# Input and first constants loaded ahead of the vector rows, group-norm fill split, and GpSimd making two of four key rows of the gate matrices

## What is computed

```python
x = first_block(x, ...)      # 2 layers: rms_norm, four branches, gates, MLP
return second_block(x, ...)  # 2 layers: modulated norm, mixer, PEER experts
```

```python
mean = jnp.mean(y, -1, keepdims=True)
var = jnp.mean(jnp.square(y - mean), -1, keepdims=True)
y = (y - mean) * lax.rsqrt(var + RWKV_GN_EPS) * hv(ln_g) + hv(ln_b)
```

```python
expert = jnp.take_along_axis(cand_idx, pos, axis=-1)
gates = jax.nn.softmax(top, axis=-1)
act = gelu(einsum('td,ted->te', hc, u[ec]))
out = einsum('te,ted->td', (gc * act), v[ec])
```

## Time and profile before

| what | us |
|---|---|
| median of 3 runs (lowest, highest) | 4231.68 (4229.45, 4231.91) |
| the profiled execution's own time | 4230.72 |
| its span in the trace | 4228.9 |
| PE busy | 4002.5 (95%) |
| DVE busy | 2099.7 (50%) |
| ACT busy | 1470.3 (35%) |
| POOL busy | 156.3 (4%) |
| mean granted clock of PE | 0.97 |

### The profile page before, as it was taken

One profiled execution on the slowest core, in us unless ns is written; L12 is line 12 of the kernel. 1 busy time (PEld: TensorE's weight loads), 2 busy tenths in 40 slices (PEclk: granted clock), 3 DMA queues, 4 the chain that ended last, 5 costly groups with the idle time before them and its releaser, 6 DMA issues.

```text
span 4228.9 us, 66869 instructions
## 1 busy us (share of the span) xinstructions
PE 4002.5 (95%) x24777; PEld 3561.0 (84%) x24777; DVE 2099.7 (50%) x4725; ACT 1470.3 (35%) x3017; POOL 156.3 (4%) x214
## 2 busy tenths in 40 slices
PE   7999989999999899899999999999989999999999
PEld 5887879979788799788887888888868878898888
DVE  1334324414343254533299555555531995555555
ACT  1222115421221163311234444444432344444444
POOL 3100100040001000000000000000000000000000
PEclk9998999999989999999999999999999999999999
DMA  4562235545512356437341555445523515554443
GB/s 129 125 177 71 58 90 150 172 122 135 167 55 61 105 160 173 102 95 195 106 137 47 182 170 175 169 170 170 151 81 107 147 46 173 174 170 170 170 173 123
DMA packets 652676, 565.62 MB, mean 134 GB/s; under 512 B 56491, under 2 KB 585786, under 8 KB 652090
## 3 DMA queue, kind: packets, MB, share of 16 engines
q1 hardware_dynamic: 652122, 559.67, 43.9%
q0 software_dynamic: 352, 3.15, 0.2%
HBM read 553.30 MB, written 9.44 MB: 133 GB/s over the span
## 4 chain that ended last, share of the span: by engine, by line
PE 89%; DVE 7%; ACT 2%; issue 1%; SPq 0%; DVEq 0%; DMA 0%; ACTq 0%
PE bank L705 22%; PE bank L1138 13%; PE bank L725 9%; PE bank L1152 6%; PE bank L1153 6%; PE bank L1151 6%; PE bank L1091 5%; PE bank L794 4%; PE bank L1127 4%; PE bank L1105 2%; PE bank L701 2%; DVE uT L2582 1%; PE bank L1081 1%; PE bank L888 1%; PE bank L898 1%; PE bank L750 1%
## 5 line engine op out<-in xcount | busy, mean ns | idle before, releaser
L705 PE MATMUL bank<-hT,ring 128*128 128x256 f32 (+1 forms) x3184 | 721.5, 387 | 23.2 <-ACT hT L1370 16.2
L705 PEld LDWEIGHTS bank<-hT,ring 128*128 128x128 f32 (+1 forms) x3184 | 609.1, 192 | 121.1 <-issue 30.9
L1138 PE MATMUL bank<-h_high,u_parts 128*128 128x256 f32 x3072 | 437.9, 285 | 0.0
L2593 DVE TENSOR_TENSOR u_parts<-bank,u_parts 128x512 fp32r<-128x512 f32 x384 | 247.0, 685 | 327.4 <-ACT u_parts L1659 327.4
L1151 PE MATMUL bank<-v_high,w_low 128*128 128x512 f32 x1024 | 406.7, 397 | 0.4 <-DVE v_low L2614 0.4
L1152 PE MATMUL bank<-v_low,w_high 128*128 128x512 f32 x1024 | 405.9, 396 | 0.0
L1153 PE MATMUL bank<-v_high,w_high 128*128 128x512 f32 x1024 | 404.8, 395 | 0.0
L1138 PEld LDWEIGHTS bank<-h_high,u_parts 128*128 128x128 f32 x3072 | 395.5, 189 | 5.9
L1360 ACT ACTIVATE arena<-bank 128x256 f32<-128x256 f32 (+2 forms) x326 | 125.1, 387 | 714.2 <-PE bank L705 545.4
L2614 DVE TENSOR_TENSOR v_low<-ring,v_high 128x512 fp32r<-128x512 f32 x512 | 336.9, 689 | 65.6 <-ACT v_high L1676 41.5
L705 PE MATMUL bank<-arena,ring 128*128 128x256 f32 (+2 forms) x1216 | 295.3, 397 | 45.6 <-DVE arena L2309 28.8
(11 more groups left out here) (391 smaller groups left out, 5847.4 us busy)
## 6 DMA issues: line engine op xcount, KB each, us to landing
ring<-in_peer_u SPq DMA_DIRECT2D x256, 512.0 KB, 4.2
ring<-in_peer_v SPq DMA_DIRECT2D x256, 512.0 KB, 3.5
ring<-in_w_in SPq DMA_DIRECT2D x132, 512.0 KB, 3.8
ring<-in_mod_w SPq DMA_DIRECT2D x96, 512.0 KB, 4.3
ring<-in_mlp_up SPq DMA_DIRECT2D x64, 512.0 KB, 4.0
ring<-in_mlp_down SPq DMA_DIRECT2D x64, 512.0 KB, 4.1
ring<-in_w_branch SPq DMA_DIRECT2D x64, 256.0 KB, 2.8
ring<-in_peer_w_q SPq DMA_DIRECT2D x32, 512.0 KB, 3.9
```

Source lines behind the costliest of these rows:

```text
L705: ins = eng.matmul(ps[0:n, 0:width], wv[:, i, :], moving(u * 8 + i), start=(u == 0 and i == 0), stop=(u == count - 1 and i == k - 1))
L1138: ins = eng.matmul(PB[6 + b][:, 0:S], u_parts[:, part, k * P:k * P + P], moving[:, k, :], start=(n == 0), stop=(n == len(products) - 1))
L2593: tt_(u_parts[:, 1, d], PB[4 + q][:, :], u_parts[:, 0, d].bitcast(F32), ALU.subtract).then_inc(sem("uL_ready"), 1)
```

## The change

Three things are changed. (1) At the start, SP loads the first 384 columns of the constants and the input, in two halves, with a semaphore of their own (`x_in`); 28 of the 49 rows are issued by SP behind them, the other 21 by ACT; the first four weight units come next, and the positions and the other constants last (`tables_in`). PE turns the input as soon as `x_in` is there, DVE copies it out bank by bank, ACT squares it, and the rows are turned last. DVE waits for the rows (`vec_ready`) only before it scales. (2) In `group_norm`, PE runs one label of fill before the second product and the rest behind it; in the RWKV branch ACT takes the root after four labels, not after all. (3) In the gate matrices, DVE compares only two of the four tokens' key rows, and POOL makes the other two, in two operations of 128x128 with a semaphore of their own (`pool_rows`). Several semaphores of another branch are also joined under one name, with the same waits.

```diff
         ANGLES, SINES, COSINES = (8, 14), (10, 16), (12, 18)
+        FILL_SQUARE, FILL_ROOT = 1, 3
...
-        SETUP = 4 + DEPTH * (12 + len(SHIFTED) + 3) + 7
+        SETUP = DEPTH * (12 + len(SHIFTED) + 3) + 7
+        FIRST_CONSTS = 3 * P
...
                 ins.then_inc(sem("gn_sum"), 1)
-                for label in fill:
+                for label in islice(fill, FILL_SQUARE):
                     project(label)
...
                 ins.then_inc(sem("gn_var"), 1)
+                for label in fill:
+                    project(label)
...
             def start_up():
-                eng.wait_ge(sem("setup_in"), pe.next("setup_in", 16 * SETUP))
+                eng.wait_ge(sem("x_in"), 16 * 3)
+                for k in range(KD):
+                    for tt in range(TT):
+                        ins = eng.transpose(PB[k // 2][:, (k % 2) * S + tt * P:(k % 2) * S + tt * P + P],
+                                            x_in[:, tt, k * P:k * P + P], C("ident"))
+                    if k % 2:
+                        ins.then_inc(sem("x_turned"), 1)
+                eng.wait_ge(sem("setup_in"), 16 * SETUP)
                 for i in range(4):
-                    eng.transpose(PB[0][:, i * P:i * P + P], rows_in[:, i, :], C("ident"))
...
+                    ins = eng.transpose(PB[6][:, i * P:i * P + P], rows_in[:, i, :], C("ident"))
...
                     eng.wait_ge(sem("one_rows"), n + (1 + base))
+                    eng.wait_ge(sem("pool_rows"), n + (1 + base))
...
+                for label in islice(fill, FILL_SQUARE + FILL_ROOT):
+                    projected(label)
+                root(gn_rs)
                 for label in fill:
                     projected(label)
-                root(gn_rs)
...
+            eng.wait_ge(sem("rows_zero"), 1)
+            layer_rows(eng, 1)
+            for b in range(4):
+                eng.wait_ge(sem("x_ready"), act.next("x_ready"))
+                eng.activation(square[:, 2 * b:2 * b + 2, :], xT[:, 2 * b:2 * b + 2, :], ACT.Square).then_inc(sem("sq_ready"), 2)
...
+            def gate_rows(l):
+
+                base = 64 * l
+                eng.wait_ge(sem("pickT_ev"), l + 1)
+                for n in range(64):
+                    b = n % 2
+                    if n >= 2:
+                        eng.wait_ge(sem("pool_rows"), n - 1 + base)
+                        eng.wait_ge(sem("gate_mm"), n - 1 + base)
+                    for j in range(2, 4):
+                        at = slice(n * 4 + j, n * 4 + j + 1)
+                        ins = ts_(one_p[:, b, j, :], C("iota"), selT[:, 1, at], None, ALU.is_equal)
+                    ins.then_inc(sem("pool_rows"), 1)
...
+            eng.dma_start(cst[:, 0:FIRST_CONSTS], io["consts"][:, 0:FIRST_CONSTS]).then_inc(sem("x_in"), 16)
+            for tt in range(TT):
+                eng.dma_start(x_in[:, tt, :], io["x"][0, tt * P:tt * P + P, :]).then_inc(sem("x_in"), 16)
             eng.wait_ge(sem("rows_zero"), 1)
+            layer_rows(eng, 0)
+            other_rows(eng)
+            load_units(4)
+            for i, name in enumerate(("positions", "positions_2")):
+                table(ipos[:, i, :], io[name].to_broadcast([P, S]))
+            table(cst[:, FIRST_CONSTS:], io["consts"][:, FIRST_CONSTS:])
...
-                    tt_(one_p[:, b, :, :], C("iota").unsqueeze(1).to_broadcast([P, 4, NKEY]),
-                        selT[:, 1, four].unsqueeze(2).to_broadcast([P, 4, NKEY]), ALU.is_equal)
+                    tt_(one_p[:, b, 0:2, :], C("iota").unsqueeze(1).to_broadcast([P, 2, NKEY]),
+                        selT[:, 1, two].unsqueeze(2).to_broadcast([P, 2, NKEY]), ALU.is_equal)
...
+            for b in range(4):
+                eng.wait_ge(sem("x_turned"), b + 1)
+                eng.tensor_copy(xT[:, 2 * b:2 * b + 2, :].rearrange("p a b -> p (a b)"), PB[b][:, :]).then_inc(sem("x_ready"), 1)
```

More of the change, by code:

```diff
@@ L1257, in gdn @@
                 eng.wait_ge(sem("go_ev"), pe.uses["go_ev"])
-                eng.wait_ge(sem("go_sq"), pe.next("go_sq"))
+                eng.wait_ge(sem("gdn_sq"), pe.next("gdn_sq"))
                 for h in range(4):
@@ L1591, in gdn @@
                     eng.wait_ge(sem("go_ev"), act.next("go_ev"))
-                eng.activation(gsq[:, 0:4, :], mix_t[:, 0:4, :], ACT.Square).then_inc(sem("go_sq"), 1)
+                eng.activation(gsq[:, 0:4, :], mix_t[:, 0:4, :], ACT.Square).then_inc(sem("gdn_sq"), 1)
                 root(gsq[:, 0:4, :])
@@ L1705, in _ @@
                 if l == 0:
+                    eng.wait_ge(sem("vec_ready"), act.next("vec_ready"))
+                    eng.activation(cond, vec[:, 3, VEC3["c"][0]:VEC3["c"][0] + 8], ACT.Silu).then_inc(sem("vec_ready"), 1)
                     sines(0)
@@ L1861, in _ @@
             condition()
+            for l in range(DEPTH):
+                gate_rows(l)
         @block.sync
@@ L2380, in gdn @@
                 eng.wait_ge(sem("gdn_scalar_in"), dve.next("gdn_scalar_in"))
[L2381 removed]
+                eng.wait_ge(sem("gdn_exps"), dve.next("gdn_exps"))
                 tt_(sp_t[:, 2, :, :], sp_t[:, 2, :, :], sp_t[:, 1, :, :], ALU.add).then_inc(sem("dve_step"), 1)
@@ L2411, in gdn @@
                 eng.wait_ge(sem("gdn_tensor_in"), dve.next("gdn_tensor_in"))
-                eng.wait_ge(sem("erow_ready"), dve.next("erow_ready"))
+                eng.wait_ge(sem("gdn_exps"), dve.next("gdn_exps", 2))
                 for b in range(8):
@@ L2573, in gate_rows @@
                 for n in range(64):
-                    b, four = n % 2, slice(n * 4, n * 4 + 4)
+                    b, two = n % 2, slice(n * 4, n * 4 + 2)
                     if n >= 2:
```

98 lines of the change are left out of this document (42 added, 56 removed).

## The result

| | before | changed |
|---|---|---|
| median | 4231.8 us | 4162.6 us |
| lowest to highest | 4229.5 to 4231.9 | 4156.6 to 4166.7 (4 executions) |
| profiled execution, its own time | 4230.7 | 4166.7 |
| its span | 4228.9 | 4164.9 |

The ratio is 0.9837, with a 95% interval of 0.9818 to 0.9856: the kernel became faster by 1.6%. The forecast was 4248 us, slower. In a second series of five executions of the changed kernel the median was 4161.8 us, with a ratio of 0.9835 (0.9821 to 0.9848). Two executions stand far apart and are left out of the ratios: one of the kernel before, of 6519.2 us (left out of the range above too), and one of five of the run with both norms as before, of 4249.5 us at a mean granted clock of 0.923.

A forecast was written before the change was run, and what follows sets the result against it. PE, busy for 95% of the span, was taken as the bound, so edits count only where it waits. 4230.7 - 14.5 - 28.8 - 5.2 - 3.4 + 69 gave 4248 us; range 4172 to 4322.

The forecast's parts named there:

- The start: Before the first projection: rows landing 7.1 us earlier plus 7.4 us of input work done beforehand, -14.5 us; bounds -10 and -15.
- The RWKV norm: Group norm of the RWKV branch, two layers: PE's 14.39 us wait goes, -28.8 us, and half clock behind it, -5.2 us.
- Retention: Retention's group norm: PE's 2.28 us wait for the root shrinks by 1.7 us per layer, -3.4 us; bounds 0 and -4.6.
- The gate stage: Gate matrices, 128 groups: period rises from 1.63 to 2.16 us as POOL pushes DVE back, +69 us; ends -29 and +153.
- DVE's own period: Gate stage: with the comparison halved, DVE needs 1.63 - 0.27 = 1.36 us per group before any push.
- POOL's comparison: Gate stage: one POOL comparison of 128x128 takes 0.60 us, set somewhat above a straight line's 0.55 us.
- The push of 0.40 us: Gate stage: each POOL operation delays DVE by its 0.60 us less 0.20, twice per group; ends 0.02 and 0.73.
- PE's period: Gate stage: PE itself needs 1.36 us of each 1.63 us group, the other 0.27 us being its wait for DVE.
- No push at all: Rival for the gate stage: POOL does not delay DVE, so the stage gains 34 us; 4145 us, chance 0.05.
- POOL slips into gaps: Rival for the gate stage: POOL gets in while DVE starts up, push 0.20, period 1.76 us, +18, 4197 us; chance 0.28.
- full exclusion: Rival for the gate stage: nothing of POOL's 0.60 us is covered, period 2.56 us, +120, 4299 us; chance 0.14.
- The test that I had named: Gate stage trace: a period under 1.98 us, POOL's operations stretched and DVE's not, would prove the forecast wrong in sign.

The follow-up runs named there:

- the first idle-work run: Changed kernel, but DVE makes all four key rows and POOL's two one-input comparisons of 128 per group go to a place nobody reads; 4182.1 us.

## Why the prediction was wrong

**The start: right in sum, with the landing mis-sized.** Predicted 7.1 for the earlier landing and 7.4 for the input; in the two traces the landing came 5.6 us earlier (14.96 against 20.51) and the way from there to the sums was 7.6 us shorter (0.9 against 8.5). By the run on one queue, 4.8 of the 5.6 are the second queue's. The issue times were right (predicted last issue 12.0 us, found 11.44; ACT's 21 from 1.44 us at the same price), the landing was not: predicted 1.44 us after the issue, found 3.52. The sum at the sums of squares was 13.2, against 14.5. Some 3 us more came by 120 us. Of these 1.4 are PE's wait behind its first projections, which shrank from 3.92 to 2.53 us. Another 1.7 are the 32 matmuls right behind that wait, which took 10.51 us (96.61 to 107.12) in place of 12.22 (111.33 to 123.55): the clock was 0.88 in the first 3.4 us there, against 0.67 in the first 3.7 us before the change, and then 0.50 for some 5 us in both. The prediction had neither.

**The RWKV norm: right.** -34.0 predicted, -33.8 found: the wait of 14.39 us and the 2.6 us at half clock went, twice. ACT's extra table load held nobody.

**Retention: the named wait shrank, and the sign was wrong.** The wait for the root shrank by 1.72 us as said. But by the prediction's own question, what comes next, it should have read on: 15 us further PE waits for DVE's copy, which a wait of 0.46 us before the change already showed to be the next bound. What counts there is DVE's chain. It started 1.6 us earlier, POOL's operations pushed it by 1.1 us more, and behind the grown wait of 3.21 us PE's clock fell, for 1.7 us more. The terms that the forecast put at nothing are the wait for DVE, the pushes and the clock behind the wait. Both ends of my bounds, 0 and -4.6, left out a loss.

**The gate stage: wrong in sign.** The sum had four terms.
- DVE's own period, 1.36 us: 1.37 by 0.34 + 1.03. Right.
- POOL's comparison, 0.60 us: 0.59 to 0.60 where DVE's two-input operation is not beside it. Right.
- The push of 0.40 us for each POOL operation: 0.06 at most. **This is the step that failed**, and alone it is 128 x 2 x 0.34 = 87 us. With 0.055 in its place the forecast's own sum for DVE, 1.37 + 2 x 0.055, gives the 1.48 us that was measured. Its words were "all of DVE's work in a group is of the kinds that were pushed". I checked that DVE's operations were like those in the earlier trace rows, and not that POOL's were. All of POOL's operations in those rows have two inputs and 256 elements; the new ones have one input and 128. The runs with idle work hold DVE fixed and change only POOL's operation: 0.42 us for a two-input one of 256, 0.15 each for two-input ones of 128, 0.17 for a one-input one of 256, and 0.03 each for one-input ones of 128. Both differences count. For the two-input form of 256, rows 9 even held in this stage: 0.42 of 0.61 us beside 0.53 of 0.73.
- PE's period, 1.36 us: 1.44. I took all of the 0.27 us of idle time as a wait for DVE, but PE cannot follow closer than that. Mis-sized by 0.08 x 128 = 10 us, on the side of the gain; with a push it does not enter the sum, since 1.48 is above it.

With 1.48 us in place of 2.16, the same sum is 4179 - 0.15 x 128 = 4160. Retention adds 5.5 to that and the start takes off 1.9: 4163.4. To the profiled execution's 4166.7 there remain 1.5 us from all other stretches and 1.8 of the gate stage, where not every group gained the full 0.15.

**The rivals.** Nearest in its mechanism was "No push at all" (4145 us, chance 0.05); it erred by PE's period, 10 us, and by the small push. "POOL slips into gaps" (4197, chance 0.28) was on the side of faster too, for a reason near the truth, but it gave DVE a push of 0.20; its +18 us is 0.13 x 128 = 17. The rule of the Trainium skill behind my full exclusion, that VectorE and GpSimd exclude each other on shared ports for the length of an instruction (SBUF — State Buffer, Who interferes with whom), goes on to name the cases: an instruction of VectorE with two inputs in SBUF contends with one of GpSimd that reads it, one with a single input outside the two-port modes does not, and whoever issues first blocks the other. The case of two inputs agrees as far as that only POOL's operation beside DVE's two-input comparison was much longer (0.90 against 0.59). The case of a single input can't be judged here: DVE's narrow operations gave way by 0.42 us beside POOL's subtraction of 256, and no run shows whether they run in a two-port mode. The order of issue does not agree: POOL's began at 2200.98, DVE's at 2201.00, and DVE's took its usual 0.41 us while POOL's was stretched. And at equal width POOL's two-input form cost DVE 0.25 us more than its one-input form, a distinction that the page does not make.

**The test that I had named.** A period under 1.98 us, with POOL's operations stretched and not DVE's, was to prove the forecast wrong in sign. The trace shows it, but for a remainder: 1.48 us, POOL's operation at 0.90, DVE's comparison at 0.41, and only 0.12 us more on its narrow operations.

## What to carry to other kernels

When contention is priced from stretched rows, match both partners by form, the intruder's too: here a one-input operation of 128 elements on POOL cost DVE 0.03 to 0.06 us, two-input ones 0.15 (128 elements) and 0.42 (256), and who yields changed with it. When work is split over two engines, give the second one what fits its price while the first one's two-input operations run (two rows of four here; three cost 37 us and one 6, in single executions and by the length of the stage alike). And where an earlier release frees a third engine, look at whose chain its work now lands on: retention's earlier root started DVE's chain 1.6 us earlier, cost 1.1 us in pushes on it, and moved PE's long wait to a place where the half clock behind it costs 1.7 us. The version with retention's fill as before keeps all the rest and is 0.6 and 1.1 us shorter in the two layers by its trace.

## What the runs showed of the hardware

- A one-input operation of 128 elements on POOL takes 0.60 us, a two-input subtraction of the same width 0.40 (the first of a pair 0.49), and one of 256 elements 0.61, against 0.93 for a one-input one of 256. The operation with a column operand was the slower form on POOL at both widths.
- Of the same two engines, the one that gives way depends on the forms: POOL's one-input operation stretched from 0.60 to 1.35 us beside two two-input operations of DVE of 0.43 and 0.68, which did not stretch. A two-input operation of POOL of 0.61 us held DVE's one-input operations up by 0.42.
- What a wait of PE costs depends on what follows it. In retention's norm PE ran at full clock behind a wait of 0.46 us and at a mean of 0.61 for 4.4 us behind one of 3.21 us, 1.7 us more for the same matmuls; the same loss behind the wait for the root was free, since PE waited for DVE later anyway.
- With two queues issuing small loads at once, each at 0.32 to 0.35 us for a load, the last of SP's landed 3.5 us after its issue; with one queue 1.55.
- The clock at the start differs between executions: the 20 us behind the first projection ran at 0.86 in the changed kernel's profiled execution and at 1.00 in that of the first idle-work run, with the same instructions there:

```profile
25.30:45.30 20.00, 19.92 (x79) 12.85 (x80) 9.67 (x26) 3.94 (x10) 8.81 (x19) 0.86 0.80 229
```

```profile
25.30:45.30 20.00, 20.00 (x94) 14.78 (x92) 8.70 (x24) 3.35 (x9) 8.84 (x19) 1.00 0.91 264
```

These are windows from 25.3 to 45.3 us: busy PE, PEld, DVE, ACT, POOL, clock, share and rate of DMA; PE ran 79 matmuls in the one and 94 in the other.
